# Expert pieces of 32 rows in four column groups of TensorE, with a delayed down product in layer 0

## The reference, cut to what matters

```python
D_MODEL = 1024; SEQ = 256; CTX_LEN = 256; DEPTH = 2
N_EXPERTS = 16; TOP_K = 2; D_EXPERT = 512

def _grouped_moe(t, router_w, router_b, w_gate, w_up, w_down):
    ...                       # two experts and their gates for each row of t
    for e in range(N_EXPERTS):
        he = jax.nn.silu(t @ w_gate[e]) * (t @ w_up[e])
        y = y + gates[:, e:e + 1] * (he @ w_down[e]).astype(jnp.float32)
    return y.astype(t.dtype)
```

## Time and profile before

| | |
|---|---|
| runs | 1302.65, 1304.79, 1305.33 us, median 1304.79 |
| profiled execution, first to last instruction | 1307.4 us |
| TensorE matmul busy | 1111.2 us, 85% of the span |
| TensorE weight loads busy | 683.2 us, 52% |
| VectorE, ScalarE, GpSimd busy | 385.9, 363.3, 87.4 us |
| moved by DMA | 317.77 MB, 243 GB/s in the mean |
| mean granted TensorE clock | 0.913 of full |

### The profile page before, as it was taken

The page is one execution under the profiler, slowest core; times in us unless marked ns, Lnnn a source line. Parts: engine busy times, 40 slices in busy tenths (PEclk is TensorE's granted clock), DMA queues, the critical chain, the costliest instruction groups (busy, mean ns, idle before and its releaser), DMA issues.

```text
span 1307.4 us, 16832 instructions
## 1 busy us (share of the span) xinstructions
PE 1111.2 (85%) x5809; PEld 683.2 (52%) x5810; DVE 385.9 (30%) x1019; ACT 363.3 (28%) x766; POOL 87.4 (7%) x145
## 2 busy tenths in 40 slices
PE   5799999998975599999998479999984987887993
PEld 2244554533435566676754257754672554454652
DVE  1366545555135000000010066655333000000012
ACT  3222345454023111222122152345231322221221
POOL 0000000000001101010001200000001110000111
PEclk9899999998996799999999779989885999988996
DMA  9920495696322269999999960230332899999953
GB/s 320 402 112 1 164 365 197 221 333 229 118 100 87 103 248 384 347 399 350 398 350 398 403 258 1 89 121 1 129 129 81 298 380 382 382 380 388 375 191 113
DMA packets 127534, 317.77 MB, mean 243 GB/s; under 512 B 5872, under 2 KB 6144, under 8 KB 127488
## 3 DMA queue, kind: packets, MB, share of 16 engines
q1 hardware_dynamic: 113680, 276.54, 57.1%
q0 software_dynamic: 12096, 40.38, 8.5%
q10 hardware_dynamic: 1712, 0.23, 0.1%
HBM read 296.68 MB, written 19.40 MB: 242 GB/s over the span
## 4 chain that ended last, share of the span: by engine, by line
PE 66%; SPq 11%; DVE 7%; DMA 7%; ACT 3%; issue 3%; POOL 1%; ACTq 1%; POOLq 0%; DVEq 0%
PE bank L570 17%; SPq L298 11%; PE bank L429 9%; PE bank L597 8%; PE bank L521 7%; PE bank L467 6%; DMA ring<-in_w_up_dram 4%; PE bank L495 3%; PE bank L372 3%; PE bank L478 3%; PE bank L560 2%; PE bank L532 1%; DVE h_t L996 1%; PE bank L438 1%; PE bank L417 1%
## 5 line engine op out<-in xcount | busy, mean ns | idle before, releaser
L570 PE MATMUL bank<-ring,h_t 128*64 128x256 f32 (+1 forms) x2176 | 316.4, 400 | 31.3 <-DMA ring<-in_w_up_dram 28.5
L570 PEld LDWEIGHTS bank<-ring,h_t 128*64 128x64 f32 (+1 forms) x2176 | 231.5, 157 | 104.5 <-issue 44.8
L597 PE MATMUL bank<-ring,h_t 128*64 128x512 f32 (+1 forms) x544 | 151.8, 597 | 17.3 <-DVE h_t L1179 14.6
L429 PE MATMUL bank<-h_t,ring 128*128 128x512 f32 (+1 forms) x320 | 117.5, 522 | 12.3 <-ACT h_t L705 12.3
L1170 DVE COPY h_t<-bank 128x256 f32<-128x256 f32 x52 | 22.1, 424 | 338.0 <-PE bank L570 338.0
L597 PEld LDWEIGHTS bank<-ring,h_t 128*64 128x64 f32 (+1 forms) x544 | 56.5, 149 | 91.2 <-issue 91.2
L429 PEld LDWEIGHTS bank<-h_t,ring 128*128 128x128 f32 x320 | 62.4, 196 | 60.2 <-issue 40.9
L996 DVE TENSOR_REDUCE h_t<-bank 128x1 f32<-128x512 f32 (+1 forms) x96 | 57.7, 601 | 106.3 <-PE bank L467 106.0
L521 PE MATMUL bank<-tokm,ring 128*128 128x512 f32 (+1 forms) x256 | 86.9, 504 | 1.1 <-DVE tokm L1018 1.1
L560 PE MATMUL bank<-cst,h_t 128*128 128x128 f32 x288 | 40.6, 286 | 38.3 <-DMA h_t<-h_rows 38.3
L977 DVE RECIPROCAL work<-work 128x512 f32<-128x512 f32 (+1 forms) x20 | 54.3, 2713 | 58.6 <-ACT work L715 58.6
(11 more groups left out here) (175 smaller groups left out, 1105.6 us busy)
## 6 DMA issues: line engine op xcount, KB each, us to landing
ring<-in_w_gate_dram SPq DMA_DIRECT2D x32, 2048.0 KB, 16.3
ring<-in_w_up_dram SPq DMA_DIRECT2D x32, 2048.0 KB, 22.4
ring<-in_w_down_dram SPq DMA_DIRECT2D x32, 2048.0 KB, 21.9
ring<-in_ada_w_dram SPq DMA_DIRECT2D x24, 2048.0 KB, 8.6
ring<-in_w_in_dram SPq DMA_DIRECT2D x8, 1536.0 KB, 21.8
h_t<-h_rows POOLq DMA_DIRECT2D x18, 512.0 KB, 7.0
ring<-in_w_out_dram SPq DMA_DIRECT2D x4, 2048.0 KB, 7.9
y_rows<-work POOLq DMA_DIRECT2D x52, 128.0 KB, 5.3
```

The costliest lines, as they stand in the source:

```text
L429: last = mm(bank[1 + i % 2][:, 0:widths[i]], qk_weights(i, k), h_t[:, k, 0:widths[i]], start=(k == 0), stop=(k == KD - 1))
L570: last = mm(o, hc_t[:, k, 0:rows], w[s][:, k, 256 * half:256 * half + 256], start=(k == 0), stop=(k == KD - 1))
L597: last = mm(o, he_t[:, k, 0:rows], wd[:, k, 512 * n:512 * n + 512], start=(k == 0), stop=(k == KF - 1))
```

## The change

- A piece is 32 rows in both layers (`CHUNK`). A product has 32 rows of output, so four stand side by side in the four column groups, each 256 columns wide: 32 products of 256 columns for gate and up, 16 for down.
- In layer 0 an expert has at least two pieces (`LEAST`), in layer 1 at least one. By the counts above that gives 4, 3, 2, 3, 3, 2, 3, 4, 2, 3, 3 and five times 2, 42 pieces in all, in layer 0, and 23 in layer 1 (1 each, but 2 for expert 7 and 3, 3, 2, 2 for the last four).
- The rows of a piece are loaded as 128 partitions of 256 columns (a quarter of a row each), so a turn is 2 transposes instead of 8, and one copy on ScalarE sorts them out. The result is 128 partitions of 256 columns too, copied once and stored in one transfer.
- In layer 0 (`expert_long`) TensorE runs down of piece g-1 behind gate and up of g and the turn of rows g+1. In layer 1 (`expert_short`) the order is that of before.
- SP refills gate and up of an expert when its last `gate_up` is done, and down when its last down product is.
- The table of pieces has 66 places instead of 26, and 15 comparisons an expert instead of 3.

```diff
-SHORT = P // 2
-CHUNK = [P, SHORT]
+CHUNK = 32
+LEAST = [2, 1]
+MAX_CHUNKS = [n * NE + 2 * t * P // CHUNK for n, t in zip(LEAST, TOK_TILES)]
...
+            def refill(l, e, a):
+                done = end_of(sp, l, e)
+                sp.wait_ge(gu_mm[l], done)
+                load_expert(l, e + 3, a, (0, 1))
+                sp.wait_ge(down_mm[l], done)
+                load_expert(l, e + 3, a, (2,))
...
+                def gate_up(g, a):
+                    w = [ring[:, 3 * a + s, :].rearrange("p (k n) -> p k n", k=KD) for s in range(2)]
+                    pe.wait_ge(hc_ready[l], g + 1)
                     for k in range(KD):
+                        for q in range(4):
+                            last = mm(bank[1][CHUNK * q:CHUNK * q + CHUNK, 0:256], hc_t[:, k, :],
+                                      w[q // 2][:, k, 256 * (q % 2):256 * (q % 2) + 256],
+                                      start=(k == 0), stop=(k == KD - 1))
...
+                def down(g, a):
+                    wd = ring[:, 3 * a + 2, :].rearrange("p (k n) -> p k n", k=KF)
+                    pe.wait_ge(het_ready[l], g + 1)
+                    pe.wait_ge(rows_ready[l], g + 1)
                     for k in range(KF):
+                        h = he_t[:, k % 2, CHUNK * (k // 2):CHUNK * (k // 2) + CHUNK]
+                        for q in range(4):
+                            last = mm(bank[4][CHUNK * q:CHUNK * q + CHUNK, 0:256], h,
+                                      wd[:, k, 256 * q:256 * q + 256], start=(k == 0), stop=(k == KF - 1))
...
+                def expert_long(e, a, turns, prev):
+                    g0, g1 = first_of(pe, l, e), end_of(pe, l, e)
+                    weights_in(a, turns, (0, 1))
+                    gate_up(g0, a)
+                    turn_rows(g0 + 1)
+                    if prev is not None:
+                        down(g0 - 1, prev)
+                    weights_in(a, turns, (2,))
+                    turn_he(g0)
+                    with pe.Fori(g0 + 1, g1) as g:
+                        gate_up(g, a)
+                        turn_rows(g + 1)
+                        down(g - 1, a)
+                        turn_he(g)
...
+                if LEAST[l] > 1:
+                    rows_turned(1)
+                    with act.Fori(0, all_chunks(act, l)) as g:
+                        gated(g)
+                        rows_turned(g + 2)
+                        row_out(g)
+                else:
+                    with act.Fori(0, all_chunks(act, l)) as g:
+                        rows_turned(g + 1)
+                        gated(g)
+                        row_out(g)
...
-                def chunk(g, rows):
+                def chunk(g):
                     pool.wait_ge(hc_turned[l], g + 2)
                     load_rows(g + 2)
                     pool.wait_ge(rows_ready[l], g + 2)
-                    row = row_of(g)
-                    for s in range(2):
-                        src = yrow[:, 512 * s:512 * s + 512] if rows == P else yrow[rows * s:rows * s + rows, 0:512]
-                        pool.dma_start(y_rows[bass.ds(row, rows), 512 * s:512 * s + 512], src
-                                       ).then_inc(rows_stored[l], 16)
+                    pool.dma_start(y_rows[bass.ds(row_of(g), CHUNK), :].rearrange("r (q c) -> q r c", q=4), yrow).then_inc(rows_stored[l], 16)
```

More of the change, by code:

```diff
@@ L61 @@
 C_TRI = C_G + GT
[L62 to L63 removed]
+C_W16 = C_TRI + (NE + 1) * NE
 C_W4 = C_W16 + NE
@@ L574, in chunk @@
[L574 to L590 removed]
+                    for j in range(2):
+                        last = turn(bank[5][:, P * j:P * j + P], hc[:, P * j:P * j + P], ident)
@@ L595, in chunk @@
-                        for n in range(2):
-                            o = bank[(4, 7)[n]][:, :] if rows == P else bank[4][rows * n:rows * n + rows, :]
-                            last = mm(o, he_t[:, k, 0:rows], wd[:, k, 512 * n:512 * n + 512],
-                                      start=(k == 0), stop=(k == KF - 1))
-                    last.then_inc(down_mm[l], 1)
-                def expert(e, a, turns):
-                    expert_chunks(pe, l, e, lambda g, rows: chunk(a, turns, g, rows))
-                    mm(bank[0][:, 0:1], ones[:, :], ones[:, 0:1], start=True, stop=True).then_inc(set_free[l][a], 1)
+                        h = he_t[:, k % 2, CHUNK * (k // 2):CHUNK * (k // 2) + CHUNK]
@@ new lines, in expert_short @@
+                def expert_short(e, a, turns, prev):
+                    g0, g1 = first_of(pe, l, e), end_of(pe, l, e)
+                    with pe.Fori(g0, g1) as g:
+                        weights_in(a, turns, (0, 1))
+                        gate_up(g, a)
+                        turn_rows(g + 1)
+                        turn_he(g)
+                        weights_in(a, turns, (2,))
+                        down(g, a)
+                expert = expert_long if LEAST[l] > 1 else expert_short
@@ L606, in experts @@
                 pe.wait_ge(route_ready, l + 1)
                 turn_rows(0)
+                expert(0, 0, 1, None)
                 with pe.Fori(0, 5) as i:
-                    for a in range(3):
-                        expert(3 * i + a, a, i + 1)
-                expert(15, 0, 6)
+                    expert(3 * i + 1, 1, i + 1, 0)
+                    expert(3 * i + 2, 2, i + 1, 1)
+                    expert(3 * i + 3, 0, i + 2, 2)
+                if LEAST[l] > 1:
+                    total = all_chunks(pe, l)
+                    turn_rows(total + 1)
+                    down(total - 1, 0)
```

204 lines of the change are left out of this document (68 added, 136 removed).

## The result

The changed kernel takes 1530.0 us (median of 4 runs, 1525.8 to 1532.9) where the kernel before takes 1304.9: a ratio of 1.172, 95% interval 1.170 to 1.175. It is slower by 225 us; the forecast was 1474 in a range of 1408 to 1545.

What follows compares the result with a forecast made beforehand. TensorE was taken to bound layer 0, and weight transfers then TensorE layer 1. Profiled span 1307.4 + 180 (layer 0) - 7 (layer 1) - 4 (behind layer 0) = 1476, median 1474 us; range 1408 to 1545.

Steps and rivals of the forecast that it cites:

- T+4.16 and T+5.74: Layer 0: T is the start of a turn of rows; forecast store at T+3.9, next load at T+5.6.
- The rival of 0.110 us: TensorE in both layers: bound by instructions at 0.110 us each, in sum about 1552 us; chance 5%.
- the two alternate: 9.6 us: Layer 0 with idle DMA engines: periods of 8.6 us and, at slow clock, 10.55 us alternate, 9.6 us.
- its own ends (+132 to +220): Layer 0's stage: +132 us if all at full clock, +220 if all slow with 0.4 us more per period.
- 16.4 x (13.85 - 9.6): Layer 0: 16.4 of 41 periods run under the weights' traffic at 13.85 us each, the others idle at 9.6.
- an estimate of 25 us beside it: Layer 0: store shape with outermost 4 costs the load behind it 1 to 2 us under load, some 25 us, unsummed.
- the earlier start: Layer 1: expert 12 starts earlier, 6 us by earlier weight streaming and 8 us by smaller row transfers.
- +2 for the last pieces: Layer 1: the last four experts' pieces take 81 us for 78.8, +2.
- the route: Layer 1's longer routing operations on 1056 elements for 416: 4.4 us, 1.6 covered by the scatter, +2.8 remaining.
- TensorE's own round: 8.1 us: Layer 1: turn, copy, table load, silu, VectorE, wake, down, gate and up sum to 8.1 us per piece.
- Behind layer 0: Stretch after layer 0: last store and gather meet idle DMA engines, losing 4 us.
- Rival 2: Layer 0: store does not hold up the load, landings under load keep 6.2 us; about 1312 us; chance 3%.

Runs made afterwards that it cites:

- the old order: The changed kernel with layer 0 in layer 1's order on TensorE and ScalarE, GpSimd's program unchanged: 1393.2 us.
- thin loads: The changed kernel with layer 0's refills reading one block of 128 rows of each weight matrix instead of all eight, or four: 1454.6 us.

## Why the prediction was right, and which terms were off

**The mechanism: right.** TensorE waits at L544 for the load of rows 41 times, the load follows the store by 1.58 us (forecast 1.5 to 2, taken 1.7), store and load are issued at T+4.16 and T+5.74 at the full clock (forecast 3.9 and 5.6), the stage's DMA share is 0.55. Moving the load out from behind the store gives 178 us back, and the old order 137.

**TensorE's work: right.** Gate and up take 3.66 us (forecast 3.45), down 1.93 (1.73). The two differ by 32 instructions and 1.73 us, 0.054 us each as forecast; what is over, 0.2 us, comes once with each group. The rival of 0.110 us is out. By the Trainium skill's figure of about 62 ns (TensorE: Matmul & The Clock Gate, Wait — 56ns, not 53.3ns?) the 32 instructions would take 1.98 us, an estimate from that page; the measured difference is below it.

**Where the 56 us between 1474 and 1530 lie.** Layer 0 is 48 us longer than forecast (+228 for +180), layer 1 with the stretch ahead of it 6 (-5 for -11). The rest of the profiled execution is 3 shorter, where nothing was forecast. And 6 us are no work at all: I set the median 2.6 us under the profiled span as in the kernel before, and here it lies 3.3 above.

**Layer 0: two terms were mis-sized, the landing of the load and the wait for a slow clock to recover.** The forecast took 2.9 us for a landing with idle DMA engines, and "idle, a slow period shortens the next wait to about 1 us, so the two alternate: 9.6 us". The stage took 522 us for the 474 forecast, just outside its own ends (+132 to +220). The run with thin loads splits the 48 us. Traffic was sized right: 68 us measured (522.0 less 453.6, with some traffic left), forecast 16.4 x (13.85 - 9.6) = 70. The periods with little traffic are 10.72 us and not 9.6: 41 x 1.12 = 46 us, nearly all of it. The timeline of that run divides them. From the issue of a load to the next turn it is 3.72 us in the mean, forecast 3.04 (2.9 and 0.14 to wake); the load is issued 7.00 us behind the turn, forecast 6.58 (the mean of 5.6 and 7.55). So:
- *The landing* has 0.68 us a period, 28 us. I had left the store's shape out of the sum, with an estimate of 25 us beside it; with the contiguous store a load needed only 2.2 to 2.4 us to the next turn in its shortest cases, with the four-dimension store 2.7 us or more. Two late loads (7.8 and 6.6 us), near the transfers for the next layer, make 8 of the 28 us. By its own run the shape costs 39 us in layer 0.
- *The clock hardly recovers*: 0.43 us a period, 17 us. Only 7 of 42 down products ran at the full clock in the changed kernel, 9 with thin loads, where half had been forecast for the idle part. The wait after a slow period was mostly 1.4 to 3 us there, not 1, and clock was lost behind it too.

This divides the time and not the causes: a longer landing brings a longer wait and with it the low clock, and each of the two runs that touched one moved the other.

**Layer 1: nearly right in sum, by two errors that cancel.** The recorded sum has a slip: 6 and 8 us for the earlier start, +2 for the last pieces and +2.8 for the route make -9.2, and -7 was written. The route stands ahead of the window, so the terms for the window itself are -12, and it measured -5.6. Expert 12 starts 174.8 us behind the first product (1400.8 less 1226.0) where it took 195.9, so 21 us earlier and not 14. From there the pieces take 94.6 us (1400.8 to 1495.4) and not 81. The step that failed is "TensorE's own round: 8.1 us": at the full clock it is 8.19, but behind the wait of 1.82 us in it the clock falls in most pieces, which makes 9.5 to 9.9 in six of nine. I had counted the load of tables and not the low clock behind it. (Expert 12 starts only 5 us earlier where the refill alone was changed; the rest of the 21 us comes with smaller transfers of rows and other pieces, which no run separates.)

**Behind layer 0: no gain.** The stretch between the layers is 268.5 us (957.5 to 1226.0) for 268.1; forecast was -4 and +2.8 for the route.

**Rival 2** (the store doesn't hold up the load, 1312 us) is what the run with the load ahead built; it took 1351.6. Missing from it was the one `yrow`: the next copy waits until the store lands.

## What to carry to other kernels

Before moving work behind other work, list what is released by its result on *every* queue: here one DMA queue served both the delayed store and the next load, and a delay of 2 us on TensorE became a chain through four engines. The delay was a gain once the load no longer stood behind it. When TensorE waits in every round of a chain (here 1.8 us in layer 1 and some 4 us in layer 0), count its work at the low clock as well, since that makes the chain longer. Change one thing at a time in a tuned kernel: one edit of this change, the earlier refill, was worth 0.8% alone, and the others hid it.

## What the runs showed of the hardware

- The clock fell behind waits of 1.82 us, though not behind each: the same 32 products took 1.93 us at a granted clock of 1.00, or 3.59 at 0.52. Adding 4.3 us of useless products to each piece made the kernel 23 us faster.
- For 128 KB from 128 partitions, a destination whose outermost dimension is 4 took 3.6 us to land at best, a contiguous one 2.0; GpSimd's instruction took 0.73 against 0.55 us, and the load queued behind it needed 5.16 against 4.37 us to the next turn in the mean.
- ScalarE's functions of one loop body were preceded by one or two loads of tables of 1.283 us in every pass; with the first pass written out ahead of the loop they were gone (97 to 52 in the program).
